# One level of Strassen's algorithm in the z and gate projections, input turns on TensorE, angles on GpSimd

## What is computed

```
u = RMSNorm(h)
q, f, i, g_hg, u_s5, z_s5, gate_hg, gate_s5 = split(u @ W_in)
HGRN2 branch: S_t = diag(f_t) S_{t-1} + (1 - f_t) i_t^T; o_t = S_t^T q_t; per-head norm; * silu(g_hg); project
S5 branch:    32 groups of 16 channels, 64 complex diagonal states each, scan over time; GELU, GLU, * silu(z_s5); project
h += W_out(sigmoid(gate_hg) * y_hg + sigmoid(gate_s5) * y_s5)
h += (p @ W_ple) * sigmoid(RMSNorm(h) @ W_ple_gate)
return RMSNorm(h)
```

## Time and profile before

| | us |
|---|---|
| median of 3 runs | 2183.71 (2183.08 to 2183.78) |
| span of the profiled execution | 2182.4 |
| TensorE matmul busy | 2166.2, 99% |
| VectorE busy | 1447.4, 66% |
| ScalarE busy | 944.9, 43% |
| GpSimd busy | 147.9, 7% |
| DMA, mean over the span | 102 GB/s |

### The profile page before, as it was taken

The page is one execution under the profiler, slowest core; times in us unless marked ns, Lnnn a source line. Parts: engine busy times, 40 slices in busy tenths (PEclk is TensorE's granted clock), DMA queues, the critical chain, the costliest instruction groups (busy, mean ns, idle before and its releaser), DMA issues.

```text
span 2182.4 us, 29586 instructions
## 1 busy us (share of the span) xinstructions
PE 2166.2 (99%) x10386; PEld 1780.9 (82%) x10386; DVE 1447.4 (66%) x3076; ACT 944.9 (43%) x1377; POOL 147.9 (7%) x269
## 2 busy tenths in 40 slices
PE   9999999999999999999999999999999999999997
PEld 6788888888888888888887888888888888888886
DVE  7700058778788788758788788456567567666756
ACT  6511135545545545543333333334444364354344
POOL 0000000000000000001111111111002001200100
PEclk9999999999999999999999999999999999999999
DMA  6422121111011011023222222366337536634632
GB/s 219 106 71 68 49 68 59 33 45 58 32 45 58 30 47 48 20 83 100 85 81 83 84 88 87 98 221 189 121 121 250 165 103 190 224 111 130 227 116 78
DMA packets 140125, 223.26 MB, mean 102 GB/s; under 512 B 38848, under 2 KB 82624, under 8 KB 140032
## 3 DMA queue, kind: packets, MB, share of 16 engines
q1 hardware_dynamic: 119952, 160.39, 23.9%
q0 software_dynamic: 20080, 61.64, 8.0%
...
## 4 chain that ended last, share of the span: by engine, by line
PE 96%; DVE 1%; DMA 1%; ACT 1%; issue 0%; SPq 0%; DVEq 0%; ACTq 0%; POOLq 0%
PE c_bank L107 29%; PE c_bank L108 29%; PE c_bank L109 29%; PE c_bank L474 1%; PE c_bank L451 1%; PE c_bank L461 1%; PE c_bank L472 1%; PE c_bank L1143 1%; PE c_bank L1146 1%; PE c_bank L1128 1%; DMA x_xs<-x_in 0%; PE c_bank L479 0%; PE c_bank L1132 0%; DMA c_raw<-w_glu_in 0%; DMA c_raw<-w_in_in 0%
## 5 line engine op out<-in xcount | busy, mean ns | idle before, releaser
L107 PE MATMUL c_bank<-u_hi,c_w_both 128*128 128x512 f32 x1216 | 484.5, 398 | 2.3 <-DVE u_lo L829 0.9
L109 PE MATMUL c_bank<-u_hi,c_w_both 128*128 128x512 f32 x1216 | 473.4, 389 | 0.0
L108 PE MATMUL c_bank<-u_lo,c_w_both 128*128 128x512 f32 x1200 | 467.5, 390 | 0.0
L107 PEld LDWEIGHTS c_bank<-u_hi,c_w_both 128*128 128x128 f32 x1216 | 228.3, 188 | 58.0 <-issue 5.9
L109 PEld LDWEIGHTS c_bank<-u_hi,c_w_both 128*128 128x128 f32 x1216 | 228.2, 188 | 48.2
L108 PEld LDWEIGHTS c_bank<-u_lo,c_w_both 128*128 128x128 f32 x1200 | 225.5, 188 | 44.2 <-issue 0.2
L1771 ACT ACTIVATE c_w_both<-c_raw 128x1024 fp32r<-128x1024 f32 x90 | 95.5, 1061 | 162.6 <-PE c_bank L109 148.8
L721 DVE STREAM_TRANSPOSE hg_ken<-hg_ke 32x128 f32<-32x128 f32 x512 | 154.8, 302 | 6.5
L1191 ACT ACTIVATE s_stage<-c_bank 128x512 f32<-128x512 f32 x80 | 47.7, 598 | 256.2 <-PE c_bank L109 251.2
L108 PE MATMUL c_bank<-t_oa_lo,c_w_both 128*128 128x512 f32 (+1 forms) x344 | 132.1, 384 | 0.0
L109 PE MATMUL c_bank<-t_oa_hi,c_w_both 128*128 128x512 f32 (+1 forms) x344 | 132.1, 384 | 0.0
...
## 6 DMA issues: line engine op xcount, KB each, us to landing
c_raw<-w_in_in SPq DMA_DIRECT2D x44, 512.0 KB, 3.8
...
c_raw<-w_o_hg_in SPq DMA_DIRECT2D x32, 512.0 KB, 3.7
c_raw<-w_out_in SPq DMA_DIRECT2D x32, 512.0 KB, 3.6
c_raw<-w_ple_gate_in SPq DMA_DIRECT2D x32, 512.0 KB, 3.5
...
```

The source lines that it names most:

```text
L107: pe.matmul(out, w_hi, u_hi, start=first, stop=False)
L108: pe.matmul(out, w_hi, u_lo, start=False, stop=False)
L109: return pe.matmul(out, w_lo, u_hi, start=False, stop=last)
```

## The change

The z and gate projections are no longer 20 blocks by 4 time tiles, but 20 units u: a pair of blocks (A's two block rows) by two time tiles (B's two block columns), and each unit is cut once more over the 1024 channels of the contraction in two halves of four (`HALF_KT`). That gives a 2 x 2 by 2 x 2 block product, done in Winograd's form of Strassen's algorithm with seven half products (`PRODS`) instead of eight. A half product is 4 x 3 = 12 matmuls (`product`). Units 0 to 9 take time tiles 0 and 1, units 10 to 19 tiles 2 and 3; the blocks go in the order of `PAIR_ORDER`, and z is in units 2, 3, 12 and 13.

- **Weight side.** Each unit needs four combinations of its four weight quarters (S1 to S4); GpSimd adds them (`sum_s3`, `sum_s1_s2`, `sum_s4`, each 128x512). Seven pieces of 128x512 per unit are rounded on ScalarE (`piece`, L254 of the new file) and split on VectorE (L259), into a ring of four; they come out of `raw` or of the sums.
- **Input side.** The combinations of the input (terms) are made during the i rows in `part_head`, on VectorE (`recover`, `combine`: 16 groups of 8 operations on 128x256), kept in DRAM by 24 stores from GpSimd's queue, and loaded over parts of `u_hi` and `u_lo` that are no longer needed: terms 0 to 3 around the end of the last head, terms 4 to 10 (all seven of the second half of the time) during units 9 and 10. A term is 128x4x512: four DMAs of 256 KB, one rounding on ScalarE, one split on VectorE. The loads of the head's first weights wait for those stores (`kept`).
- **Output side.** The seven products go to banks `sum_a` (two, in turn), `sum_b` and `sum_d`. ScalarE copies a bank as it stands in the middle of the accumulation (`snapshot`, 4 per unit), VectorE adds (`add_c11`, `add_c12`, `add_c22`), ScalarE takes the sigmoids out of `stage`. Products 2, 4, 5 and 6 wait for the snapshot behind product 0, 2, 3 and 4.
- **S5 branch.** `turn_inputs` becomes two transposes of 128x128 on TensorE behind product 5 of a unit, and one copy on ScalarE (`copy_turned`). `angles` becomes ten operations on GpSimd, each waiting for the one before. `states` is cut in three (`turn_back`, `scans`, `turn_forward`) and stands ahead of `matrices`. `last_step` runs behind products 0, 2, 4 and 6 of unit 0.

```diff
+    TERMS = [(0, 2), (0, 3), (0, 4), (0, 6)] + [(1, i) for i in range(PRODS)]
+    SUM_OF = {2: (2, 3), 3: (1, 2), 4: (0, 1), 5: (2, 4)}
...
+    def load_term(self, sp, m):
+        half, i = self.TERMS[m]
+        if m < 2:
+            sp.wait_ge(self.head_proj, 3 * (NT * (HEADS - 1) + 2))
+            for sem in self.kept:
+                sp.wait_ge(sem, 16 * 12)
+        elif m < 4:
+            sp.wait_ge(*self.term_lo.at(m - 1))
+        else:
+            sp.wait_ge(*self.prod_done.at(PRODS * 9 + i + 1))
+        src = self.a["terms"][half, :, :, :, self.SLOT[i]]
+        for k in range(HALF_KT):
+            sp.dma_start(self.raw_term(m)[:, k].rearrange("p (h n) -> p h n", h=2), src[:, k]).then_inc(self.term_in[m % 7].sem, 16)
...
+    def sum_s4(self, pool, u):
+        raw, out = self.w.raw, self.sums
+        pool.wait_ge(*self.piece_lo.at(PRODS * u + 3))
+        pool.tensor_tensor(out[:, self.S2], raw[:, 0, HALF_KT:], out[:, self.S2], ALU.add).then_inc(self.sums_done.sem, 1)
...
+            for u in range(NQ):
+                p = u - AHEAD
+                if u < NQ - 1:
+                    quads.load_block_a(sp, u + 1)
...
+                if u == 0:
+                    quads.load_term(sp, 2)
+                    quads.load_term(sp, 3)
+                if u in MAKE:
+                    load_u(p)
+                if u in USE:
+                    fill_intra(p)
+                if u == 9:
+                    quads.load_term(sp, 4)
+                    quads.load_term(sp, 5)
+                if u < NQ - 1:
+                    quads.load_block_b_high(sp, u + 1)
...
+                if u == 9:
+                    for m_ in range(6, len(quads.TERMS)):
+                        quads.load_term(sp, m_)
...
+                link(pool.tensor_scalar(a1, nn[:], f_hi[:, p:p + 1], None, ALU.mult))
+                link(pool.tensor_scalar(a2, a1, MAGIC, MAGIC, ALU.add, ALU.subtract))
+                link(pool.tensor_tensor(a1, a1, a2, ALU.subtract))
+                link(pool.tensor_scalar(a2, nn[:], f_lo[:, p:p + 1], None, ALU.mult))
+                link(pool.tensor_tensor(a1, a1, a2, ALU.add))
+                link(pool.tensor_scalar(a2, a1, MAGIC, MAGIC, ALU.add, ALU.subtract))
+                link(pool.tensor_tensor(sin, a1, a2, ALU.subtract))
+                link(pool.tensor_scalar(a1, sin, 0.25, None, ALU.add))
+                link(pool.tensor_scalar(a2, a1, MAGIC, MAGIC, ALU.add, ALU.subtract))
+                pool.tensor_tensor(cos, a1, a2, ALU.subtract).then_inc(ang_done, 1)
...
+            for u in range(NQ):
+                if u:
+                    store(u - 1, C21)
+                    store(u - 1, C22)
...
-            slots(pool, body)
+                if u in GELU:
+                    store_y(u - AHEAD - 2)
+                if u in MAKE:
+                    angles(u - AHEAD)
+                if u < NQ - 1:
+                    quads.sum_s3(pool, u + 1)
+                    quads.sum_s1_s2(pool, u + 1)
+                store(u, C11)
+                store(u, C12)
+                if u < NQ - 1:
+                    quads.sum_s4(pool, u + 1)
+            store(NQ - 1, C21)
+            store(NQ - 1, C22)
...
+            def product(u, i):
+                q = PRODS * u + i
+                pe.wait_ge(*quads.piece_lo.at(q + 1))
+                if (u // 10, i) in quads.TERMS and u % 10 == 0:
+                    pe.wait_ge(*quads.term_lo.at(quads.TERMS.index((u // 10, i)) + 1))
+                if i == 0:
...
+                else:
+                    pe.wait_ge(*snapped.at(4 * u + {2: 1, 4: 2, 5: 3, 6: 4}[i]))
...
+                hi, lo = quads.ring(q)
+                ks, at = quads.term_at(i)
+                b_hi, b_lo = quads.terms(u // 10)
+                for kk_ in range(HALF_KT):
+                    k = ks.start + kk_
+                    start, stop = i in (0, 1, 3) and kk_ == 0, i in (1, 5, 6) and kk_ == HALF_KT - 1
+                    pe.matmul(out[:], hi[:, kk_], b_hi[:, k, at], start=start, stop=False, skip_group_check=True)
+                    pe.matmul(out[:], hi[:, kk_], b_lo[:, k, at], start=False, stop=False, skip_group_check=True)
+                    ins = pe.matmul(out[:], lo[:, kk_], b_hi[:, k, at], start=False, stop=stop, skip_group_check=True)
+                ins.then_inc(prod_done.sem, 1)
+
+            def turn_inputs(p):
+
+                pe.wait_ge(xz_done, p + 1)
+                if p >= 2:
                     pe.wait_ge(gelu_done, p - 1)
+                for k in range(2):
+                    ins = pe.transpose(turned[:, k * P:(k + 1) * P], X[:, k].rearrange("p j c -> p (j c)"), c["ident"][:])
+                ins.then_inc(x_turned.sem, 1)
...
-            slots(pe, body)
...
+                snapshot(u, 0, sum_a(u), C11)
+                piece(u, 0)
+                if u in GELU:
+                    act.wait_ge(msb_done, min(p, PAIRS) * 2)
+                    gelu(p - 2)
...
+                snapshot(u, 2, sum_a(u), C12)
+                piece(u, 2)
...
+                snapshot(u, 3, sum_d, C22)
+                piece(u, 3)
...
+                snapshot(u, 4, sum_a(u), C21)
+                piece(u, 4)
...
+                if u in MAKE:
+                    sine(p)
+                sigmoid(u, C11)
+                piece(u, 5)
...
+                if u in MAKE:
+                    copy_turned(p)
+                sigmoid(u, C12)
...
+                    last_step(0)
                 if use:
                     taps()
+                    turn_back()
+                piece(u, 0)
+                if use:
+                    scans()
+                if u == 0:
+                    quads.split_term(dve, 2)
+                add_c11(u)
+                piece(u, 1)
+                if u == 10:
+                    quads.split_term(dve, 9)
+                if use:
+                    turn_forward()
+                if u == 10:
+                    quads.split_term(dve, 10)
+                piece(u, 2)
+                if u == 0:
+                    last_step(1)
+                if u == 9:
+                    quads.split_term(dve, 4)
                 if make:
                     matrices()
-                if z:
-                    gated(b, 0)
-                if is_at(b, 0):
-                    last_step(0)
-                else:
-                    split_weights(b + 1, 1 - r)
-                if is_at(b, 1):
+                piece(u, 3)
...
+                piece(u, 4)
...
+                gated(u, C11)
+                add_c12(u)
+                add_c22(u)
+                piece(u, 5)
+                if u == 9:
+                    quads.split_term(dve, 6)
+                gated(u, C12)
...
+                piece(u, 6)
+                if u == 9:
+                    quads.split_term(dve, 7)
+                gated(u, C21)
+                gated(u, C22)
+                if u == 0:
```

746 lines of the change are left out of this document (508 added, 238 removed).

## The result

| | before | changed |
|---|---|---|
| median, us (4 runs each) | 2183.39 (2182.88 to 2183.78) | 2280.28 (2278.27 to 2282.16) |
| ratio | | 1.044 (1.043 to 1.046) |
| span of the profiled execution | 2182.4 | 2276.5 |

The change makes the kernel 4.4% slower, where 2171 us had been forecast, 0.6% faster. The span is 106.5 us over the 2170.0 of the sum.

What follows compares the result with a forecast made beforehand. TensorE, busy 99% of the span, was taken as the bound. 2182.4 - 54.4 + 8 + 8 + 11 + 2 + 13 = 2170.0, with 1.3 us outside the span 2171 us, 0.6% faster; range 2150 to 2260.

Steps and rivals of the forecast that it cites:

- the sum: Whole kernel: the profiled 2182.4 us with all forecast savings and costs added gives a span of 2170.0 us.
- What bounds the kernel, and what is removed: Projections: TensorE sets the time; 1920 matmuls become 1680, 240 x 0.227 = 54.4 us less.
- GpSimd ... is hidden with 1 us in hand, at nothing: GpSimd in each unit: angles done at 13.6 us, next unit's sums about 17.5, wanted at 18; no cost.
- rival 1: GpSimd's and VectorE's SBUF reads exclude each other: X 4.8 us later in 16 units, 2248 us; chance 0.35.
- It waits 0.5 us, in 16 units: 8 us more: TensorE behind product 5: X ready at 17.1 us, wanted at 16.6; 8 us more (0 to 20).
- Rival 2: GpSimd alone is slow, 1 us per angle operation: 1 to 3 us a unit, about 2200 us; chance 0.13.
- Unit 0: First unit: term 2 lands late, is split at 951, product 4 waits; 11 us more (4 to 17).
- Unit 1: Behind unit 0: SP waits for the last output before it loads on; 2 us more (0 to 5).
- Units 9 and 10: Seven term splits on VectorE delay X; both units take 60.7 us instead of 47.4, 13 us more (6 to 22).
- The loads keep ahead: Term loads in units 9 and 10: each waits for its product of unit 9 and has a unit's time.
- The range: Whole kernel: 2150 to 2260 us, leaving out half of rival 3 (transitions covered, 2150 us) and rival 1's upper third.

Runs made afterwards that it cites:

- e6: Changed kernel with all GpSimd arithmetic of the units (ten angle operations and four weight sums) replaced by memsets of the same sizes: 2189.5 us.
- b1: Kernel before, with extra GpSimd operations (tensor_tensor, tensor_scalar, memsets) on otherwise unused tiles in five blocks: 2195.0 us, against 2182.0 before on the same chip.
- e3: Changed kernel with the four tensor_tensor operations of the angles made one-input tensor_scalar of the same size on GpSimd: 2286.4 us.
- e9: Changed kernel without the loads, roundings and splits of terms 4 to 10 in units 9 and 10: 2270.3 us.
- e8: Changed kernel with SP's two next w_glu loads issued ahead of the loads of silu(z) at the start of the last part: 2278.0 us.

## Why the prediction was wrong, point by point

- **What bounds the kernel, and what is removed: right.** Units 18 and 19, without S5 inputs to make, take the 40.3 us of their matmuls; e6's units have TensorE busy for 23.14 of 23.19 us against 23.1. The 54.4 us are really saved.
- **"GpSimd ... is hidden with 1 us in hand, at nothing": the step that failed.** It was wrong twice. GpSimd's own prices: 0.45 was taken for a tensor_scalar of 128x256, and b1 has 1.02 (the row that it leaned on, 0.29 us for a select of 128x128, gives 0.58 by proportion already); a sum was put at 1.2, and b1 has 1.36 (the prediction's proportion, 2048 elements in 4497 ns, gives 1.12 for 512, not 1.2); the angles end 18.4 us into a unit, not 13.6. And what it takes from VectorE: rival 1. Together they cost 91 us (2280.3 to 2189.5 in e6), 72 in the 13 units, 9 in units 9 and 10, 10 in units 0 to 2. In the 13 units only the second reaches TensorE: its wait is for X, and VectorE has no gap over 0.3 us on the way to X (1111.69 to 1127.22 in the unit shown), so it waits there for nothing that GpSimd makes. GpSimd's own length is the next chain, 1.0 us behind; it shows in unit 2, where TensorE waits 2.2 us for the turned copy, and in e3.
- **"It waits 0.5 us, in 16 units: 8 us more".** The chain from product 0 to X was priced at 12.7 us; it is 12.2 without GpSimd and 15.5 with it. It had been seen that X has no cover at all; a step of which one says that "the cover is nil" ought not to carry a term of 0.5 us in the likeliest case.
- **Rival 1** had the mechanism, the place and nearly the size: 4.8 us a unit forecast, 5.5 over e6's 23.2 measured. Of these 3.7 us are X's delay, and 1.8 the clock behind the wait (8.3 us from the turns to the next unit instead of 6.5), which rival 1 left out. That the sum came near is partly luck: it added the six tensor_scalar at their full length, which take little, and had no clock. Its 2280 for S1 and S2 in the same stretch is luck as well, since both fall there in units 11 and 14 only, of the 13. It said "GpSimd's reads"; the full length is lost to tensor_tensor alone, and one-input reads take the smaller part (`matrices` 6.1 us in e3 against 5.4 in e6). It deserved the larger chance: the trace of before could not show it, but the page that the prediction quotes could. The Trainium skill, SBUF — State Buffer, says in its section "Who interferes with whom" that a VectorE instruction with two SBUF inputs contends with a GpSimd instruction that reads SBUF, and in its section "Terms" that the loser is blocked for the whole instruction. The blocking agrees with b1 beside tensor_tensor (0.78 and 1.33 us for an operation of 0.29). Beside tensor_scalar, which reads SBUF too, it does not: 0.31 to 0.39 in block 4 and at most 0.65 in block 17, beside operations of 1.6 us.
- **Rival 2** gave 2200 with 1 us per angle operation, and that price was right. Its cost alone was not seen alone: e3, with angles 0.8 us longer still, is 6 us above the changed kernel with rival 1's wait nearly gone.
- **Unit 0: right.** 35.8 us against 35; term 2 was split at 951.5 (forecast 951). Unit 1: 22.7 against 21.1.
- **Unit 2: a term that was missing.** VectorE's and ScalarE's parameters of the S5 part stand at the end of unit 1, 9 us in a chain (993.27 to 1002.2), with the snapshot of product 0 behind them; TensorE waits 5.9 us. By the program's order the same chain had a block's slack in the kernel before, and the ring of four pieces has not; no run tests that alone. It adds to the late X of that unit; 4.3 of the 12 us remain in e6.
- **Units 9 and 10: 13 us forecast**, 19.6 in e6 (66.0 us for the two, against 2 x 23.2) and 9 more with GpSimd's arithmetic; beside that arithmetic, e9 has the terms at 16.6. "The loads keep ahead" failed for term 4.
- **The seam to the last part: a term that was missing**, 10.7 us, of which e8 gives 8 back. I had looked at what starts the change's stretch and not at what its end hands over.
- **The range** of 2150 to 2260 did not hold 2280. It cut off the upper third of rival 1, and rival 1's own 2248 was built on a base that was too low by itself: e6, without GpSimd's cost, has a span of 2187.6 us where the sum had 2170.0.
